# Moving both gates and the norm's offset to GpSimd and the norm's scale to ScalarE in the last stage of a hybrid decoder layer

## What is computed

```
attn  = sum over 3 dilations of softmax(lse) * out          # 512 columns
a_out = attn * silu(ga)
ms    = mean(o_b^2) per head of 128
b_out = o_b * rsqrt(ms + eps) * norm_g * silu(gb)           # 512 columns
z     = ALPHA * x + concat(a_out, b_out) @ w_out            # 1024 columns
y     = (z - mean(z)) * rsqrt(var(z) + eps) * ln_g + ln_b
```

## Time and profile before

| | |
|---|---|
| Median of 3 runs | 1799.24 us (1798.23 to 1801.51) |
| Profiled execution | 1798.6 us, span 1796.9 us |
| Busy over the span | PE 1608.5 us (90%), PEld 1445.8, DVE 788.8 (44%), ACT 473.7 (26%), POOL 193.6 (11%) |
| Mean granted TensorE clock | 0.94 of full speed |
| Last stage | 1518 to 1796.9 us |

### The profile page before, as it was taken

The page is one execution under the profiler, slowest core; times in us unless marked ns, Lnnn a source line. Parts: engine busy times, 40 slices in busy tenths (PEclk is TensorE's granted clock), DMA queues, the critical chain, the costliest instruction groups (busy, mean ns, idle before and its releaser), DMA issues. The chain is left out here.

```text
span 1796.9 us, 26047 instructions
## 1 busy us (share of the span) xinstructions
PE 1608.5 (90%) x9834; PEld 1445.8 (80%) x9834; DVE 788.8 (44%) x2016; ACT 473.7 (26%) x1335; POOL 193.6 (11%) x181
## 2 busy tenths in 40 slices
PE   5999999989899989999899994699989996298997
PEld 4999999985687767877699994699989996177775
DVE  4100000006222232211179882356556663589995
ACT  4011111113001132222201121356555654312110
POOL 0000000001500010000000001564141000011111
PEclk9999999998999999999869996799999998599999
DMA  7988888888938678856302213954662103655641
GB/s 244 280 250 253 255 253 254 251 281 243 273 101 303 221 269 255 266 179 220 106 1 92 77 45 96 242 129 112 144 144 66 50 26 102 254 178 183 219 160 41
DMA packets 175150, 319.68 MB, mean 178 GB/s; under 512 B 14676, under 2 KB 114452, under 8 KB 168724
## 3 DMA queue, kind: packets, MB, share of 16 engines
q1 hardware_dynamic: 146860, 177.96, 31.3%
q10 hardware_dynamic: 21248, 108.93, 19.3%
q0 software_dynamic: 6928, 31.31, 6.8%
HBM read 255.01 MB, written 143.89 MB: 222 GB/s over the span
## 5 line engine op out<-in xcount | busy, mean ns | idle before, releaser
L220 PE MATMUL acc<-xhi,whi 128*128 128x424 f32 (+1 forms) x640 | 229.0, 358 | 23.6 <-DVE xlo L200 23.6
L220 PE MATMUL acc<-xlo,whi 128*128 128x424 f32 (+1 forms) x640 | 228.6, 357 | 0.0
L220 PE MATMUL acc<-xhi,wlo 128*128 128x424 f32 (+1 forms) x640 | 228.3, 357 | 0.0
L705 PE MATMUL nacc<-nwhi,nxhi 128*128 128x512 f32 (+1 forms) x544 | 219.2, 403 | 8.8 <-DVE nwlo L454 8.8
L1268 ACT ACTIVATE a_prob<-a_prob,a_stage 128x256 f32<-128x256 f32 (+1 forms) x384 | 174.3, 454 | 181.3 <-DVE a_stage L1243 180.7
L705 PE MATMUL nacc<-nwlo,nxhi 128*128 128x512 f32 (+1 forms) x544 | 214.3, 394 | 0.0
L705 PE MATMUL nacc<-nwhi,nxlo 128*128 128x512 f32 (+1 forms) x544 | 214.3, 394 | 0.0
L1243 DVE CUSTOM_DVE_ANT_0 a_prob<-a_s_ps,a_bias 128x256 f32<-128x256 f32 (+1 forms) x384 | 125.4, 364 | 187.9 <-PE a_s_ps L1306 187.1
L1330 PE MATMUL a_o_ps<-a_v,a_probT 128*128 128x64 f32 x1200 | 157.1, 269 | 8.4 <-DMA a_v<-projN 7.6
L1306 PE MATMUL a_s_ps<-a_khi,a_q 128*128 128x256 f32 (+1 forms) x384 | 157.9, 418 | 6.9 <-POOL a_klo L1215 6.9
L1330 PEld LDWEIGHTS a_o_ps<-a_v,a_probT 128*128 128x128 f32 x1200 | 150.0, 193 | 9.8 <-issue 9.3
(11 more groups left out here) (169 smaller groups left out, 2581.6 us busy)
## 6 DMA issues: line engine op xcount, KB each, us to landing
projT<-stage SPq DMA_DIRECT2D x16, 1056.0 KB, 4.9
out_kwin_s<-in_cache_kT ACTq DMA_DIRECT2D x8, 2048.0 KB, 14.0
spare<-in_xT SPq DMA_DIRECT2D x32, 512.0 KB, 7.8
projN<-nstage SPq DMA_DIRECT2D x32, 512.0 KB, 5.4
qg<-in_cache_kT ACTq DMA_DIRECT2D x8, 2048.0 KB, 11.0
d_vlow<-in_cache_v ACTq DMA_DIRECT2D x8, 2048.0 KB
a_raw<-projT POOLq DMA_DIRECT2D x32, 512.0 KB, 9.6
out_kwin_s<-in_cache_kT ACTq DMA_DIRECT2D x8, 2032.0 KB, 18.5
```

The costliest lines, as they stand in the source:

```text
L220: mm = pe.matmul(acc[:, j, 0:n], w[:, u, k], x[:, k, c0:c0 + n], start=(k == 0 and a == 0), stop=(k == KD - 1 and a == 2))
L705: mm = pe.matmul(acc[0:m, n % 2], x[:, u, k, 0:m], w[:, k, g * H:(g + 1) * H], start=(k == 0 and b == 0), stop=(k == KD - 1 and b == 2))
```

## The change

Only the last stage changes, and only GpSimd's, ScalarE's and VectorE's lists; TensorE's and SP's lists stay as they are.

- GpSimd now multiplies o_b by its gate for the whole tile at once (128x512), then by the inverse rms, broadcast over each head, and then the attention part by its gate. So it is GpSimd that signals mix_done.
- The norm's second pass is split: ScalarE multiplies by the inverse deviation (scale_y), GpSimd adds ln_b (add_bias) and signals y_done. The inverse deviation gets two halves.
- VectorE loses the four per-head products, the gate product and the second pass of the norm. It waits for its own first pass of tile t-1 before it overwrites z.
- In turn t, GpSimd does recurrent_part(t), attention_part(t), inverse_rms(t+1), add_bias(t-3), inverse_deviation(t-2). ScalarE does exponentials(t), squares(t+1), scale_y(t-3), round_mix(t).

```diff
@@ -1357,7 +1357,7 @@
-        st, mv, vr, rstd = sb("m_st", [P, 2, 6]), sb("m_mv", [P, 2]), sb("m_vr", [P, 1]), sb("m_rstd", [P, 1])
+        st, mv, vr, rstd = sb("m_st", [P, 2, 6]), sb("m_mv", [P, 2]), sb("m_vr", [P, 1]), sb("m_rstd", [P, 2])
...
@@ -1450,6 +1451,12 @@
                     nc.scalar.activation(mhi[:, u, 4:8, 0:n], tp[:, 1, :, 0:n], ACT.Copy,
                                          scale=ngt[:, 0:1]).then_inc(mhi_done, 1)
 
+                def scale_y(t):
+                    n, w = rows_in[t], t % 2
+                    act.wait_ge(yc_done, t + 1)
+                    act.wait_ge(rstd_done, t + 1)
+                    nc.scalar.activation(yt[0:n, w], yt[0:n, w], ACT.Copy, scale=rstd[0:n, w:w + 1]).then_inc(ys_done, 1)
+
                 squares(0)
                 exponentials(0)
                 for k in range(4):
@@ -1463,7 +1470,11 @@
                         exponentials(t)
                     if t + 1 < NALL:
                         squares(t + 1)
+                    if t >= 3:
+                        scale_y(t - 3)
                     round_mix(t)
+                for t in range(NALL - 3, NALL):
+                    scale_y(t)
 
             @block.gpsimd
             def _(pool):
@@ -1479,47 +1490,68 @@
                         pool.wait_ge(mix_done, t - 1)
                     nc.gpsimd.tensor_tensor(rs[0:n, u], ms[0:n, u], half[0:n], ALU.pow).then_inc(rs_done, 1)
 
+                def recurrent_part(t):
+                    n, u = rows_in[t], t % 2
+                    pool.wait_ge(landed[u], 16 * NLD * (t // 2 + 1))
+                    if t >= 2:
+                        pool.wait_ge(t_done, t - 1)
+                    b = mix[0:n, u, H:2 * H]
+                    nc.gpsimd.tensor_tensor(b, ob[0:n, u], gate[0:n, u, 1], ALU.mult).then_inc(og_done, 1)
+                    pool.wait_ge(og_done, t + 1)
+                    pool.wait_ge(rs_done, t + 1)
+                    bh = b.rearrange("p (h d) -> p h d", h=HB)
+                    nc.gpsimd.tensor_tensor(bh, bh, rs[0:n, u].unsqueeze(2).to_broadcast([n, HB, DB]), ALU.mult).then_inc(b_done, 1)
+
+                def attention_part(t):
+                    n, u = rows_in[t], t % 2
+                    a = mix[0:n, u, 0:H]
+                    if t < NTL:
+                        pool.wait_ge(a_done, t + 1)
+                    pool.wait_ge(b_done, t + 1)
+                    nc.gpsimd.tensor_tensor(a, a if t < NTL else mixa[0:n], gate[0:n, u, 0], ALU.mult).then_inc(mix_done, 1)
+
                 def inverse_deviation(t):
-                    n = rows_in[t]
+                    n, w = rows_in[t], t % 2
                     pool.wait_ge(vr_done, t + 1)
-                    nc.gpsimd.tensor_tensor(rstd[0:n], vr[0:n], half[0:n, 0:1], ALU.pow).then_inc(rstd_done, 1)
+                    if t >= 2:
+                        pool.wait_ge(ys_done, t - 1)
+                    nc.gpsimd.tensor_tensor(rstd[0:n, w:w + 1], vr[0:n], half[0:n, 0:1], ALU.pow).then_inc(rstd_done, 1)
+
+                def add_bias(t):
+                    n, w = rows_in[t], t % 2
+                    pool.wait_ge(ys_done, t + 1)
+                    nc.gpsimd.tensor_tensor(yt[0:n, w], yt[0:n, w], lbb[0:n], ALU.add).then_inc(y_done, 1)
 
                 inverse_rms(0)
-                inverse_rms(1)
-                for t in range(2, NALL):
-                    inverse_rms(t)
-                    inverse_deviation(t - 2)
-                inverse_deviation(NALL - 2)
-                inverse_deviation(NALL - 1)
+                for t in range(NALL + 3):
+                    if t < NALL:
+                        recurrent_part(t)
+                        attention_part(t)
+                    if t + 1 < NALL:
+                        inverse_rms(t + 1)
+                    if t >= 3:
+                        add_bias(t - 3)
+                    if 2 <= t < NALL + 2:
+                        inverse_deviation(t - 2)
 
             @block.vector
             def _(dve):
                 tt, stt = nc.vector.tensor_tensor, nc.vector.scalar_tensor_tensor
-                AS = 8
+                AS = 7
 
                 def combine(t):
                     n, u = rows_in[t], t % 2
                     r = slice(0, n)
-                    sample = t == NTL
                     dve.wait_ge(landed[u], 16 * NLD * (t // 2 + 1))
-                    if not sample:
-                        nmx = pt[r, u, :, :, DA + 1]
-                        tt(mn[r], nmx[:, 0], nmx[:, 1], ALU.min).then_inc(mn_done, 1)
-                        dve.wait_ge(mn_done, 2 * t + 1)
-                        tt(mn[r], mn[r], nmx[:, 2], ALU.min).then_inc(mn_done, 1)
-                        dve.wait_ge(mn_done, 2 * t + 2)
-                        tt(wd[r], mn[r].unsqueeze(1).to_broadcast([n, NC, HA]), nmx, ALU.subtract).then_inc(d_done, 1)
-                    dve.wait_ge(rs_done, t + 1)
+                    nmx = pt[r, u, :, :, DA + 1]
+                    tt(mn[r], nmx[:, 0], nmx[:, 1], ALU.min).then_inc(mn_done, 1)
+                    dve.wait_ge(mn_done, 2 * t + 1)
+                    tt(mn[r], mn[r], nmx[:, 2], ALU.min).then_inc(mn_done, 1)
+                    dve.wait_ge(mn_done, 2 * t + 2)
+                    tt(wd[r], mn[r].unsqueeze(1).to_broadcast([n, NC, HA]), nmx, ALU.subtract).then_inc(d_done, 1)
                     if t >= 2:
                         dve.wait_ge(t_done, t - 1)
-                    for h in range(HB):
-                        c = slice(h * DB, (h + 1) * DB)
-                        last = stt(mix[r, u, H + h * DB:H + (h + 1) * DB], ob[r, u, c], rs[r, u, h:h + 1], gate[r, u, 1, c],
-                                   ALU.mult, ALU.mult)
                     a = mix[r, u, 0:H]
-                    if sample:
-                        tt(a, mixa[r], gate[r, u, 0], ALU.mult).then_inc(mix_done, 1)
-                        return
                     dve.wait_ge(wexp_done, t + 1)
                     tt(wd[r], wexp[r], pt[r, u, :, :, DA], ALU.mult).then_inc(a_step, 1)
                     dve.wait_ge(a_step, AS * t + 1)
@@ -1538,15 +1570,15 @@
                     av = a.rearrange("p (h d) -> p h d", h=HA)
                     tt(av, pt[r, u, 0, :, 0:DA], pt[r, u, 1, :, 0:DA], ALU.add).then_inc(a_step, 1)
                     dve.wait_ge(a_step, AS * t + 7)
-                    tt(av, av, pt[r, u, 2, :, 0:DA], ALU.add).then_inc(a_step, 1)
-                    dve.wait_ge(a_step, AS * t + 8)
-                    tt(a, a, gate[r, u, 0], ALU.mult).then_inc(mix_done, 1)
+                    tt(av, av, pt[r, u, 2, :, 0:DA], ALU.add).then_inc(a_done, 1)
 
                 def residual(t):
                     n, w = rows_in[t], t % 2
                     r = slice(0, n)
                     dve.wait_ge(x_landed[w], 16 * (t // 2 + 1))
                     dve.wait_ge(z_done, t + 1)
+                    if t >= 1:
+                        dve.wait_ge(yc_done, t)
                     for g in range(2):
                         c = slice(g * H, (g + 1) * H)
                         ins = stt(z[r, c], xt[r, t % 4, c], ALPHA, z_ps[r, w, g], ALU.mult, ALU.add)
@@ -1570,9 +1602,6 @@
                     if t == 0:
                         dve.wait_ge(const, 16 * 4)
                     stt(yt[r, w], z[r], mv[r, 0:1], lgb[r], ALU.subtract, ALU.mult).then_inc(yc_done, 1)
-                    dve.wait_ge(yc_done, t + 1)
-                    dve.wait_ge(rstd_done, t + 1)
-                    stt(yt[r, w], yt[r, w], rstd[r], lbb[r], ALU.mult, ALU.add).then_inc(y_done, 1)
 
                 def rest_of_mix(t):
                     n, u = rows_in[t], t % 2
@@ -1592,7 +1621,8 @@
                 combine(1)
                 rest_of_mix(1)
                 for t in range(2, NALL):
-                    combine(t)
+                    if t < NTL:
+                        combine(t)
                     residual(t - 2)
                     rest_of_mix(t)
                     normalise(t - 2)
```

More of the change, by code:

```diff
@@ L1369, in merge_and_project @@
             sem(f"m_{n}") for n in ("a_step", "mix_done", "t_done", "mhi_done", "mlo_done", "z_done"))
-        zr, bn_done, mv_done, vr_done, rstd_done, yc_done, y_done = (
-            sem(f"m_{n}") for n in ("zr", "bn_done", "mv_done", "vr_done", "rstd_done", "yc_done", "y_done"))
+        zr, bn_done, mv_done, vr_done, rstd_done, yc_done, ys_done, y_done = (
+            sem(f"m_{n}") for n in ("zr", "bn_done", "mv_done", "vr_done", "rstd_done", "yc_done", "ys_done", "y_done"))
+        a_done, og_done, b_done = sem("m_a_done"), sem("m_og_done"), sem("m_b_done")
         NLD = 4
```

## The result

The changed kernel takes 1804.4 us (median of 20 runs, 1800.7 to 1809.9) against 1798.9 us of the kernel before on the same chips: a ratio of 1.0031, interval 1.0023 to 1.0039. It is 5.4 us slower. The direction and the range held; the forecast of 12 us was more than twice the loss.

The account below looks back on a forecast made before the run. VectorE was taken to set the last stage's pace, TensorE close behind. Ring rounds +7.8, first tiles +1.6 and end +2.2, in all +11.6 us, gave a median of 1811 us, range 1795 to 1820.

Parts of the forecast that it names:

- the ring: Last stage: load, squares, root calls, addition, store and next load wait on each other; 14.0 us a round against 13.29 before.
- last transposes to the end: Program end: the last tile's root, scaling on ScalarE and addition on GpSimd finish later, +2.2 us.
- The 1.6: First tiles of the last stage: +3.0 us if GpSimd holds VectorE, -2.5 if not, weighted three to one.
- Load so 8.4: Load of each tile: mean 7.4 us plus 1.0 for the store in front; 8.4 us, from 6.8 to 9.4.
- The rest of the ring: Per round besides the load: squares 1.3, root calls 1.5, addition 2.35 + 0.05, store issue 0.34 + 0.04; together 5.6 us.
- its own case: The forecast that rounds are near 14 us: 1804 to 1818 us, loads 7.9 to 8.9 us, VectorE held or not; chance 0.5.
- The port: GpSimd calls and VectorE instructions with two SBUF inputs exclude each other; up to 2.4 us a round on VectorE.
- The loop: Path from transposes to transposes through VectorE and GpSimd's gate: 11.4 us, or 13.8 if GpSimd's products hold VectorE.
- costs nothing: GpSimd's addition of the norm's offset meets only VectorE instructions reading at most one SBUF tensor, so it adds no time.
- Rival 1: VectorE held by GpSimd sets the last stage's rounds, 13.8 us, loads not lengthened: +11 us, 1810; chance 0.2.
- The reverse direction of the exclusion: VectorE waiting for a long GpSimd call; no earlier row showed it; bounds 0 and the whole call.
- The clock: TensorE's clock, granted in full (1.00) with 1.25 us pauses; nothing counted for pauses of 2 us.

Follow-up runs that it names:

- e4: e2 with a store of only 16 of the 1024 columns, SP's order kept; 1789.2 us, ratio 0.9941 to the kernel before.
- e2: Changed kernel with GpSimd's two recurrent-branch products over 4 columns instead of 512, store order kept; 1799.6 us, ratio 1.0001 to the kernel before.
- e1: Changed kernel with SP's store one turn later (tile t-3 instead of t-2 behind the loads); 1802.7 us, ratio 1.0018 to the kernel before.
- e5: Kernel before with only the norm's second pass moved to ScalarE and GpSimd, gates left on VectorE, SP's order kept; 1797.0 us, ratio 0.9985.
- e8: Kernel before with only the gates' three products moved to GpSimd, norm left on VectorE; 1806.4 us, ratio 1.0037.
- e6: e5 with the store one turn later (tile t-3 behind the loads); 1796.1 us, ratio 0.9979 to the kernel before.
- e11: Changed kernel with the later store and the recurrent products of tile t+1 taken early, behind its inverse rms; 1806.1 us, ratio 1.0048 to the kernel before.
- e7: e6 with one more wait, so GpSimd's addition starts only after VectorE's residual, beside the statistics; 1786.4 us, ratio 0.9924 to the kernel before.
- e3: Changed kernel with both the later store and the recurrent products over 4 columns; 1786.6 us, ratio 0.9926 to the kernel before.

## Why the prediction was right in direction and wrong in size

By the starts of the transposes, the 5.3 us split like this:

| stretch | forecast | measured |
|---|---|---|
| tile 0 to 3, before the ring closes | +1.6 | +1.7 (49.85 against 48.19) |
| tile 3 to 15, the ring's rounds | +7.8 | +1.3 (13.40 against 13.29) |
| last transposes to the end | +2.2 | +2.3 (34.7 against 32.4) |

The agreement of the first line is luck in part. The 1.6 is a weighted mean of +3.0, if VectorE is held, and -2.5, if not. It was held, and the cost was 1.7: the round of tile 0 grew by 1.8 (22.06 against 20.24; forecast 2.5), and the next two rounds by nothing (27.79 against 27.95; forecast +0.5).

**The step that failed is "Load so 8.4".** The 11 waited loads of the steady rounds took 7.86 us on average. The store's share was nearly right (0.88 measured in e4 against e2, forecast 1.0), the base was not: 7.4 was the mean of one load seen as a wait, 8.0, and one of 6.8. Before, loads were visible as waits only where they landed late, in four of 11 steady rounds, so the 8.0 was picked by its lateness; the base is 7.1 (e4). The rest of the ring was good: 5.6 forecast, 5.49 measured. Ring 7.86 + 5.49 = 13.35 against a mean round of 13.40. The mis-sized load is worth 11 x 0.54 = 5.9 us of the 6.5 that this stretch is off, and the rest of the ring 1.2; together a little more than the miss, because the mean round, 13.40, is a little longer than the ring. The lower end that the prediction gives for its own case, 1804, doesn't follow from its terms either: with loads of 7.9 and VectorE never held they make 1801.

**The port** was sized too high as well, without a price, because the ring was as long. The hold was 1.6 to 1.85 us a round, not 2.4: GpSimd's two products need 1.29 and 1.04 us, and VectorE is held for a part of each only, 0.7 to 1.1 us by the first and 0.7 to 0.9 by the second. The loop is 13.30 (e1), not 13.8.

**How the ring reaches the path** was told by half. The prediction has late squares delay ScalarE's rounding, and an addition that "costs nothing". In the changed kernel VectorE's m_mlo does start late in five of the 12 rounds, by 0.06 to 1.0 us. But in eight (from tile 4 to 11, and from 12 to 13) the ring's addition runs on for 0.2 to 0.4 us after L1604 has started, and that sets the path. L1604 then ends 1.08 to 1.10 us after the addition, and the next transposes start 9.2 us after it. The rows above have one: the addition ends at 1621.65, L1604 at 1622.73, and the transposes start at 1630.86. These eight rounds are the ring's, 13.06 to 14.25 and 13.45 on average. In the other four the addition ends within 0.05 us of L1604's start, and the loop alone gives 13.30. So the ring acts through the port, and each sets part of the rounds. Rival 1 had the mechanism of those four; but e2 shows that the ring by itself is no shorter. That the norm's part and the gates' part each do no more than break even or lose (e5, e8) is the same finding by parts.

**The reverse direction of the exclusion**, which no row of before showed, is shown now in e1, e6 and e11. Each lengthened VectorE instruction reads two tensors from SBUF and ends with the GpSimd call, or up to its own time behind it; L1578 in e7 reads one and isn't lengthened. All of these agree with the rule of the Trainium skill ("SBUF — State Buffer", section "Who interferes with whom"). The prediction gave it three parts in four, and only for the start. There it is the eight weight differences, 1456 ns each against 1216 before, 1.9 us in all.

**The clock** stayed at 1.00 from tile 3 on in the changed kernel, with pauses of 1.0 to 2.25 us ahead of the transposes; to count nothing for it was right.

**The prices** on the path were within 0.1 us: a product 1.26 (forecast 1.25), the addition 2.40 (2.35), the scaling 1.14 (1.1), and the floor without ring and port 12.12 (12.1). The end came as worked out:

```profile
1789.92 1.27 DVE L1604 SCALAR_TENSOR_TENSOR m_y<-m_z,m_mv,m_lgb 64x1024 f32<-64x1024 f32 x1
1790.08 1.52 POOL L1518 TENSOR_TENSOR m_rstd<-m_vr,m_half 64x1 f32<-64x1 f32 x1 [5.75 <-DVE m_vr L1595]
1791.69 1.15 ACT L1458 ACTIVATE m_y<-m_y,m_rstd 64x1024 f32<-64x1024 f32 x1 [9.85 <-POOL m_rstd L1518]
1792.91 2.33 POOL L1523 TENSOR_TENSOR m_y<-m_y,m_lbb 64x1024 f32<-64x1024 f32 x1 [1.32 <-ACT m_y L1458]
```

**Where the gain went.** VectorE's bound was lifted, as e3 and e7 show with rounds of 12.1. Of the 12 x 1.2 = 14 us that this is worth, the changed kernel got nothing: GpSimd's products took up to 1.85 of VectorE's 3.1 us back, GpSimd's gate product takes 1.27 us on the path in place of VectorE's 0.69, and the order of stores and loads closed a ring as long. What stays open is why loads with the same bytes ahead spread so far, from 7.3 to 9.4 us in e5, and which of them come late.

## What to carry to other kernels

Before work is moved off a full engine, follow its result into the queues behind it: a store that now waits for a slower engine, ahead of loads in one queue, turned a free transfer into a ring of 13.4 us against a floor of 12.1. Work moved from VectorE to GpSimd belongs beside VectorE instructions that read at most one SBUF tensor; elsewhere either engine can be held (VectorE's 0.69 us became 2.72, GpSimd's 1.03 became 2.63), and one added wait that places it (e7 against e6) was worth 10 us. Take a transfer's usual time from many loads, not from the one that shows up as a wait, since those are the late ones.

## What the runs showed of the hardware

- GpSimd's product with a broadcast operand (L1503) is faster than that of two full tensors: 1.04 us against 1.29 for 128x512. The prediction had one price for both.
- A VectorE instruction of 0.17 us can take 1.26 us beside a GpSimd product (e1); one of 0.69 us took 2.72 beside the 128x1024 addition (e6).
- A GpSimd call of 4 elements per partition, 1.03 us alone, took 2.63 us beside VectorE's 128x1536 product (e6).
- After TensorE had stood 2.35 to 2.5 us, the next round ran at a mean granted clock of 0.87 to 0.89 in four cases of five and took 13.25 to 13.48 us without a pause, against 11.93 at 1.00 in the fifth (e6). In the changed kernel pauses of up to 2.25 us left it at 1.00.
